# Exchanging transposed exponents between partition quadrants: per head through HBM, or per query block from SBUF to SBUF

## What is computed

```python
def attend_block(args):
    n, qn = args
    kw = lax.dynamic_slice_in_dim(kp, n * BLOCK, BLOCK + 2 * WINDOW, axis=1)
    vw = lax.dynamic_slice_in_dim(vp, n * BLOCK, BLOCK + 2 * WINDOW, axis=1)
    s_win = jnp.einsum('bqkgd,bjkd->bkgqj', qn, kw).astype(jnp.float32) * scale
    s_ctx = jnp.einsum('bqkgd,bjkd->bkgqj', qn, k_ctx).astype(jnp.float32) * scale
...
    logits = jnp.concatenate([sink_logits(sink, s_win.shape[:-1]), s_ctx, s_win], axis=-1)
    p = jax.nn.softmax(logits, axis=-1)
...
    return (jnp.einsum('bkgqj,bjkd->bqkgd', p_ctx, v_ctx)
            + jnp.einsum('bkgqj,bjkd->bqkgd', p_win, vw))
```

## Time and profile before

| | |
|---|---|
| median of three runs | 1405.53 us |
| profiled execution | 1405.84 us |
| its span in the trace | 1404.1 us |
| TensorE busy | 1367.9 us, 97% |
| VectorE busy | 864.5 us, 62% |
| ScalarE busy | 517.5 us, 37% |
| GpSimd busy | 74.8 us, 5% |
| the four heads | about 386 to 646 us |
| TensorE busy in them | 248.6 of 260 us |

### The profile page before, as it was taken

One profiled execution on the slowest core, in us unless ns is written; L12 is line 12 of the kernel. 1 busy time (PEld: TensorE's weight loads), 2 busy tenths in 40 slices (PEclk: granted clock), 3 DMA queues, 4 the chain that ended last, 5 costly groups with the idle time before them and its releaser, 6 DMA issues.

```text
span 1404.1 us, 19111 instructions
## 1 busy us (share of the span) xinstructions
PE 1367.9 (97%) x7258; PEld 1142.4 (81%) x7258; DVE 864.5 (62%) x1327; ACT 517.5 (37%) x798; POOL 74.8 (5%) x145
## 2 busy tenths in 40 slices
PE   5999999999999999999999999999999999999998
PEld 2788888888878788878888888888888888887887
DVE  6545655656787787776645776677665334474435
ACT  5323422234564645454222442212363223333332
POOL 0001111111000000000110100000000000010000
PEclk9999999999999999999999999999999999999999
DMA  9996567666676757687766666356533333365333
GB/s 384 407 396 250 180 206 254 191 186 198 201 208 163 192 172 178 176 230 261 236 198 192 195 192 194 92 173 195 160 91 102 103 91 105 105 198 181 111 90 120
DMA packets 103490, 265.35 MB, mean 189 GB/s; under 512 B 13536, under 2 KB 41200, under 8 KB 102000
## 3 DMA queue, kind: packets, MB, share of 16 engines
q1 hardware_dynamic: 81792, 185.72, 42.5%
q0 software_dynamic: 19936, 73.38, 16.7%
q10 hardware_dynamic: 1680, 5.10, 1.0%
HBM read 245.78 MB, written 18.38 MB: 188 GB/s over the span
## 4 chain that ended last, share of the span: by engine, by line
PE 83%; DMA 6%; DVE 5%; issue 2%; SPq 2%; ACT 2%; DVEq 0%; ACTq 0%
PE ps L1578 83%; DMA blocks<-cond_row 2%; DMA modchunk<-blocks 2%; DMA kvmem<-in_ctxT 1%; SPq L431 1%; DVE w_lo L972 1%; DVE pt_lo L1288 1%; DMA raw<-in_mod 1%; ACT w_hi L543 1%; DVE cond_row L1275 1%; DVE tmp L1265 0%; SPq L389 0%; DVE tmp L1098 0%; DVE kvmem L1160 0%; DVE kvmem L1265 0%
## 5 line engine op out<-in xcount | busy, mean ns | idle before, releaser
L1578 PE MATMUL ps<-h_hi,w_hi 128*128 128x512 f32 x1592 | 621.0, 390 | 2.1 <-DVE h_lo L1053 1.2
L1578 PE MATMUL ps<-h_lo,w_hi 128*128 128x512 f32 x1592 | 618.5, 389 | 0.0
L1578 PE MATMUL ps<-h_hi,w_lo 128*128 128x512 f32 x1592 | 618.2, 388 | 0.0
L972 DVE TENSOR_TENSOR w_lo<-raw,w_hi 128x1024 fp32r<-128x1024 f32 x206 | 252.2, 1224 | 371.2 <-ACT w_hi L543 370.3
L543 ACT CAST w_hi<-raw 128x1024 fp32r<-128x1024 f32 x206 | 216.1, 1049 | 598.8 <-PE ps L1578 598.7
L1578 PEld LDWEIGHTS ps<-h_hi,w_hi 128*128 128x128 f32 x1592 | 299.0, 188 | 65.8 <-issue 5.4
L1578 PEld LDWEIGHTS ps<-h_hi,w_lo 128*128 128x128 f32 x1592 | 298.9, 188 | 62.0
L1578 PEld LDWEIGHTS ps<-h_lo,w_hi 128*128 128x128 f32 x1592 | 299.0, 188 | 58.5
L978 DVE CUSTOM_DVE_ANT_0 modchunk<-modchunk,cond_row 128x1024 f32<-128x1024 f32 x128 | 154.6, 1219 | 19.9 <-DMA modchunk<-in_modb 19.7
L489 POOL DMA_DIRECT2D modchunk<-in_modb x128 | 67.6, 528 | 828.3 <-DVE modacc L978 811.9
L744 ACT ACTIVATE tmp<-tmp,stat 128x513 f32<-128x513 f32 (+1 forms) x24 | 18.7, 780 | 43.1 <-DVE stat L1265 43.0
(11 more groups left out here) (231 smaller groups left out, 1356.1 us busy)
## 6 DMA issues: line engine op xcount, KB each, us to landing
raw<-in_weights SPq DMA_DIRECT2D x208, 512.0 KB, 3.6
modchunk<-in_modb POOLq DMA_DIRECT2D x128, 512.0 KB, 4.7
raw<-in_mod SPq DMA_DIRECT2D x32, 512.0 KB, 9.2
modchunk<-in_mod SPq DMA_DIRECT2D x16, 512.0 KB, 7.5
cond_row<-in_mod SPq DMA_DIRECT2D x16, 512.0 KB, 9.5
blocks<-cond_row SPq DMA_DIRECT2D x24, 320.0 KB, 5.4
blocks<-cond_row SPq DMA_DIRECT2D x24, 256.0 KB, 2.9
modchunk<-blocks SPq DMA_DIRECT2D x64, 80.0 KB, 3.6
```

The source lines that it names most:

```text
L972: nc.vector.tensor_tensor(low, src, high.bitcast(F32), ALU.subtract).then_inc(lo_ready, 1)
L1578: return nc.tensor.matmul(out, lhsT, rhs, start=start, stop=stop, skip_group_check=True)
```

## The change

The transposed exponents of the three steps of a block are collected in one buffer (`cond_row`) and exchanged once a block, straight from SBUF to SBUF into a second one (`modchunk`). There are 16 transfers, one for each pair of source and target quadrant, of 32 partitions by 1536 bytes (blocks 0 and 3) or 1920 bytes (blocks 1 and 2). The four with equal source and target go on GpSimd's queue, the other twelve on SP's. The copy in HBM goes. High parts are made three at a time in slots 4, 7, 10 and 13, low parts three at a time in slots 5, 8, 11 and 14. With one buffer of each kind, `turn_blocks` of a block's first step waits until the transfers of the block before have landed, and in slots 6 and 12 it now stands behind the weights' low part. The inverse sums have one buffer instead of two.

```diff
-TURN_LAG = 3
-TURN_SLOTS = 3
+HIGH_SLOTS = (4, 7, 10, 13)
+LOW_SLOTS = (5, 8, 11, 14)
+ROW_SLOTS = (4, 7, 10, 13)
+POOL_MOVES = [(a, a) for a in range(4)]
+SP_MOVES = [(a, j) for j in range(4) for a in range(4) if (a, j) not in POOL_MOVES]
...
+        def block_source(n, a, j):
+
+            return block_runs(n, cond_row)[a * QUADRANT:(a + 1) * QUADRANT, j]
+
+        def block_target(n, a, j):
+
+            return block_runs(n, chunk_flat)[j * QUADRANT:(j + 1) * QUADRANT, a]
+
+        def moves_landed(eng, b):
+
+            eng.wait_ge(pt_landed, 16 * len(SP_MOVES) * (b + 1))
+            eng.wait_ge(pt_landed_pool, 16 * len(POOL_MOVES) * (b + 1))
...
-            def store_blocks(i, k):
-                g, cols = i * STEPS + k, key_tiles(k) * P
-                sp.wait_ge(turned, g + 1)
-                sp.dma_start(turn_scratch[g % 4, :, 0:cols], blocks_out[g % 2][:, 0:cols]).then_inc(written[g % 2], 16)
-
-            def fetch_blocks(i, k):
...
+            def move_blocks(i, n):
+                b = i * BLOCKS + n
+                sp.wait_ge(turned, (b + 1) * GQA)
+                if b:
+                    sp.wait_ge(pt_ready, b * GQA)
+                for a, j in SP_MOVES:
+                    sp.dma_start(block_target(n, a, j), block_source(n, a, j)).then_inc(pt_landed, 16)
...
                     if k < STEPS and k % GQA == GQA - 1:
+                        move_blocks(i, k // GQA)
                         store_inverse(i, k // GQA)
-                    if 3 <= k <= STEPS and k % GQA == 0:
-                        fetch_inverse(i, k // GQA - 1)
...
+            for b in range(KV_HEADS * BLOCKS):
+                pool.wait_ge(turned, (b + 1) * GQA)
+                if b:
+                    pool.wait_ge(pt_ready, b * GQA)
+                for a, j in POOL_MOVES:
+                    pool.dma_start(block_target(b % BLOCKS, a, j), block_source(b % BLOCKS, a, j)).then_inc(pt_landed_pool, 16)
...
-                if g >= 2:
-                    dve.wait_ge(written[g % 2], 16 * (g // 2))
-                nc.vector.transpose(blocks_out[g % 2][:, 0:cols].rearrange("p (j t c) -> p j t c", j=4, c=QUADRANT),
+                if k % GQA == 0 and g:
+                    moves_landed(dve, g // GQA - 1)
+                nc.vector.transpose(turned_blocks(k),
...
-                    if k > TURN_LAG:
-                        for n in {NEXT_SCORES: (STEPS - 2, STEPS - 1), NEXT_SCORES + 1: ()}.get(k, (k - TURN_LAG - 1,)):
-                            turned_lo(i, n)
+                    if k in LOW_SLOTS:
+                        for j in range(GQA):
+                            turned_lo(i, LOW_SLOTS.index(k) * GQA + j)
...
-                    if k < STEPS and (k or first):
+                    if k < STEPS and k % GQA:
                         turn_blocks(i, k)
                     if k < STEPS and k % GQA == GQA - 1:
                         invert_sums(i, k // GQA)
                     if k in UNIT_SLOTS:
                         lo(i + G_Z, UNIT_SLOTS.index(k) + 2)
+                    if k < STEPS and k % GQA == 0 and (k or first):
+                        turn_blocks(i, k)
                     if k in BLOCK_SLOTS:
                         block_out(i, BLOCK_SLOTS.index(k))
```

More of the change, by code:

```diff
@@ L277, in build @@
         chunk_flat = modchunk[:].rearrange("p a n -> p (a n)")
[L278 to L281, removed]
+        inverse_row = kv_part(k_rope + 5 * P + QUADRANT // 2, [GQA * P])
         key_raw = kv_part(k_rope, [2, COLS])
@@ L313, in turned_tiles, with block_runs, turned_blocks, landed_tiles @@
             return dst[:, 0:tiles, j * P:(j + 1) * P].rearrange("p t (a c) -> p t a c", c=QUADRANT)
-        def landed_tiles(i, k):
-            return blocks_in[(i * STEPS + k) % TURN_SLOTS][:, 0:key_tiles(k) * P].rearrange("p (a t c) -> p t a c", a=4, c=QUADRANT)
+        def block_runs(n, mem):
+            return mem[:, 0:GQA * key_tiles(n * GQA) * P].rearrange("p (a x) -> p a x", a=4)
+        def turned_blocks(k):
+            run = key_tiles(k) * QUADRANT
+            return block_runs(k // GQA, cond_row)[:, :, k % GQA * run:(k % GQA + 1) * run].rearrange("p a (t c) -> p a t c", c=QUADRANT)
+        def landed_tiles(k):
+            run = key_tiles(k) * QUADRANT
+            return block_runs(k // GQA, chunk_flat)[:, :, k % GQA * run:(k % GQA + 1) * run].rearrange("p a (t c) -> p t a c", c=QUADRANT)
+        def block_source(n, a, j):
[5 more added lines that the diff above has]
+            eng.wait_ge(pt_landed_pool, 16 * len(POOL_MOVES) * (b + 1))
         S_END = 6 * 512 - 256
@@ L352, in build @@
         exp_done, turned = sem("exp_done"), sem("turned")
-        written = [sem(f"written{i}") for i in range(2)]
-        pt_landed = [sem(f"pt_landed{i}") for i in range(TURN_SLOTS)]
+        pt_landed, pt_landed_pool = sem("pt_landed"), sem("pt_landed_pool")
         inverse_ready = sem("inverse_ready")
         inverse_written = [sem(f"inverse_written{i}") for i in range(2)]
-        inverse_landed = [sem(f"inverse_landed{i}") for i in range(2)]
+        inverse_landed = sem("inverse_landed")
         row_stored, row_back = sem("row_stored"), sem("row_back")
@@ L750, in turned_hi @@
                 g = i * STEPS + k
[L751 to L754, removed]
+                if k % GQA == 0:
+                    moves_landed(act, g // GQA)
+                    if g:
+                        act.wait_ge(pv_done, g // GQA)
+                nc.scalar.copy(turned_tiles(k, pt_hi), landed_tiles(k)).then_inc(pt_hi_ready, 1)
             def last_swap(i, k):
@@ L785, in attention @@
                         hi(i + G_Z, UNIT_SLOTS.index(k) + 2)
[L786 to L787 removed]
+                    if k in HIGH_SLOTS:
+                        for j in range(GQA):
+                            turned_hi(i, HIGH_SLOTS.index(k) * GQA + j)
                     if i < 2:
@@ L1287, in turned_lo @@
                 dve.wait_ge(pt_hi_ready, i * STEPS + (k + 1))
-                nc.vector.tensor_tensor(turned_tiles(k, pt_lo), landed_tiles(i, k), turned_tiles(k, pt_hi).bitcast(F32),
+                nc.vector.tensor_tensor(turned_tiles(k, pt_lo), landed_tiles(k), turned_tiles(k, pt_hi).bitcast(F32),
                                         ALU.subtract).then_inc(pt_ready, 1)
@@ L2066 @@
     out = nc.dram_tensor("out", (2, KT // 2, P, SEQ), F32, kind="ExternalOutput").ap()
-    blocks = nc.dram_tensor("blocks", (4, P, 5 * P), F32, kind="Internal").ap()
     inverses = nc.dram_tensor("inverses", (2, P, GQA), F32, kind="Internal").ap()
     row = nc.dram_tensor("row", (1, D), F32, kind="Internal").ap()
-    build(nc, *args, out, blocks, inverses, row)
+    build(nc, *args, out, inverses, row)
     result = run_bass_kernel_spmd(nc, [arrays], core_ids=[0]).results[0]["out"]
```

36 lines of the change are left out of this document (11 added, 25 removed).

## The result

The kernel after takes 1481.16 us (median of four runs, 1479.29 to 1486.85) against 1405.1 us before: a ratio of 1.054, 95% interval 1.051 to 1.058. It is slower, as forecast, but by 76 us instead of 40, and the time lies outside the range.

The account below looks back on a forecast made before the run. TensorE work plus its few waits was taken to bound the kernel. Twelve block intervals of 17.3 us, 207.6 against 165.4, lose 42 us; 2 come back: +40, 1445 us, range 1425 to 1472.

Parts of the forecast that it names:

- Eleven more issues ... at 0.44 that is 4.8 us: First queue after each closing transpose: eleven issues before the last transfer begins, 4.8 us of a 6.9 us wait.
- high end of 0.48: Slow case: 0.48 us an issue and 3.7 us landings give a 9.0 us wait, 2.1 more per interval: 1470.
- were not spread by it beyond 2.00 us: Earlier fetches also wrote quadrants, four issues taking at most 2.00 us, so the issue sets the pace.
- since nothing else stands in the queue then: Reason for taking 2.0 us from issue to landing for the block's last transfer on the first queue.
- the rest of those stretches stays: Between heads no transpose waits for landings, so apart from the 2 us counted back those stretches keep their time.
- 2 us back: Between heads: two or three slot 12 waits for low parts, 0.9 us each, go, winning 2 us.
- hidden wait: Rival 1: VectorE doesn't wait long and TensorE's ten waits go; at best 1394 us. Chance 0.05.
- half hidden: Rival 2: block interval of 13.8 to 14.2 us, offset by 2 us between heads; no change, 1405. Chance 0.04.
- Rival 4: Landings as slow as in the crowded queue, over 9 us of wait: above 1470. Chance 0.06.
- clock rival: Rival 3: TensorE's granted clock falls in the new intervals' gaps of about 3.8 us; 1460 to 1560. Chance 0.1.
- the granted clock falls in the gaps: One of three conditions under which the prediction called itself wrong; TensorE's gaps in the new block intervals.
- The other signs: Expected profile: twelve VectorE idles of 3 to 5 us, TensorE maxima waits of 3 to 4, closing transposes 16 to 19 apart.

Follow-up runs that it names:

- short rows: Kernel after, with the first queue's 12 transfers moving only 16 floats (64 bytes) of each row instead of 384 or 480: 1475.61 us, ratio 1.050.
- work in TensorE's gaps: Kernel after, plus ten extra matmuls into an unread PSUM bank before the scores of steps 5, 8 and 11 of each head: 1483.23 us, ratio 1.056.
- eight on each queue: Kernel after, with eight transfers on the first queue and eight on GpSimd's instead of 12 and 4: 1459.91 us, ratio 1.040.
- source in HBM: Kernel after, with the first queue's 12 transfers reading weight rows in HBM instead of the transposed exponents: 1453.35 us, ratio 1.034.
- four on the first queue: Kernel after, with four transfers on the first queue and four on GpSimd's, eight of 16 quadrant pairs not exchanged: 1419.21 us, ratio 1.011.
- the kernel before with the value product later: Kernel before, with the value product in slots 6, 9 and 12 behind two gate projection parts instead of one: 1403.82 us, ratio 0.998.

## Why the prediction was right and wrong

**Right: the sign and its mechanism.** The wait stood where the prediction put it, twelve times, and TensorE waited for the maximum behind it. The cut to four issues, the HBM source and the split over two queues each moved the interval by about what the chain says: forecast 14.7, 17.3 with 0.44 us an issue, and 17.0, measured in head 1 as 15.4, 17.7 and 17.3 us. The sums show it best. In the kernel after and in the runs that leave the place of the wait alone, the part up to the waiting transpose and the part behind it are, added over the twelve intervals:

| | wait part | rest |
|---|---|---|
| kernel after | 112.9 us | 122.6 us |
| short rows | 106.6 us | 122.6 us |
| work in TensorE's gaps | 114.2 us | 122.7 us |
| eight on each queue | 92.0 us | 122.7 us |
| source in HBM | 90.3 us | 122.7 us |
| four on the first queue | 57.3 us | 123.2 us |

The wait halves and the rest stays: every microsecond of wait is one of the interval. The rest was forecast as 12 x 10.4 = 124.8 us.

**Wrong: the term "Eleven more issues ... at 0.44 that is 4.8 us".** It was sized from issues whose one side is HBM, the nearest rows, and its high end of 0.48 was taken from the same rows. From SBUF to SBUF an issue takes 0.63 us with the gap, so eleven take 6.9. That is 2.1 us in each of twelve intervals, 25 of the 37 us of the span that were missed. 17.3 + 2.1 = 19.4 us an interval; the mean measured is 235.5 / 12 = 19.6. The landing was sized right: 2.0 us taken, 1.98 measured.

This term alone did not break the range. Its upper end allowed a wait of 9.0 us, for another reason (landings of 3.7 us), and stood at 1470; eleven waits of about 9.1 us would have fitted in it by luck. What took the time beyond it are the two that follow, which the prediction put at nothing or at a gain.

The statement that four fetches "were not spread by it beyond 2.00 us" holds for the lines of the earlier trace rows only. Right behind the store of 471.25 that is shown there, four of them took 3.06 us:

```profile
471.69 3.06 SPq L431 DMA_DIRECT2D modchunk<-blocks  x4
```

That these were slow for having a quadrant as target isn't shown; the first queue's other traffic is a rival.

**Wrong: landings of 2.0 us, "since nothing else stands in the queue then".** That holds for the first queue; the other queues were left out. In head 3 one interval, from 683.52 to 707.49 us, took 24.0 us, with a wait of 13.0. ScalarE's queue loads 1 MB of x there. Transfers from 676 to 700 us (KB each, us to landing):

```profile
main<-in_xT ACTq DMA_DIRECT2D x1, 1024.0 KB, 8.0
modchunk<-cond_row SPq DMA_DIRECT2D x12, 60.0 KB, 4.9
```

The landings took 4.9 us beside it instead of 2.0. The wait is 4 us longer than the 9.1 of the others, 4 us of the missed. With short rows, the same load issued 1.9 us after the closing transpose as here, the wait was 9.5 us, so the delay comes with the bytes of the exchange. That the load is the cause fits this but was not tried by moving it.

**Wrong: "the rest of those stretches stays", and 2 us back.** Outside the intervals 6.7 us were lost. 3.8 of them lie between the heads, and 2.8 of these are work of TensorE that slid there out of the intervals. That it slid because TensorE had run at half clock around each gap is supported by the run with work in the gaps, as shown there, and not tried by itself. Where the waits were shortest, with four issues, the stretches between heads took 71.5 us, 3.5 less than before: a gain as the prediction counted it is there when nothing overlays it. The 2.0 us after the last head can't be told from scatter, since that part took 769 to 775 us in all runs and 774.1 in the kernel before with the value product later; one wait of 3.8 us for low parts stands in it. With these 8.7 us, the 25 and the 4, the missed 37 us of the span are covered to within 1 us.

**The rivals.** A hidden wait and a half hidden one did not happen. Rival 4 gave the right side of the range, above 1470 with a wait over 9 us, for the wrong reason: all landings but those of one interval were fast. The clock rival did happen, as the lowered digits of the clock in the page and the mean of 0.91 over the heads show, and so did the sign "the granted clock falls in the gaps" that the prediction named as one of being wrong. Its price was wrong. It counted 1 us of scores on the chain each time, or TensorE's whole work at half clock. In seven of the twelve intervals the scores ran at half clock, in the other five the clock fell only a microsecond or two after TensorE was back, and with the clock mostly full again the time stayed. The first is an example of those five, scores at full speed after nearly 4 us:

```profile
404.50 0.44 PE L1596 MATMUL ps<-k_hi,q_hi 128*128 128x384 f32 x1 [3.90 <-DVE stat L1281]
```

The rule of the Trainium skill (TensorE: Matmul & The Clock Gate, "Part 1: The HAM clock gate") that the clock falls to 1.2 GHz after an idle stretch agrees with this trace: 0.50 after the gap of 4.1 us. A fall can still be nearly free, when another engine's chain is longer.

**The other signs.** Closing transposes were 17.7 to 24.0 us apart (16 to 19 forecast), the stalls on VectorE 5 to 11 us (3 to 5 forecast, low because the wait itself was). TensorE's gaps before the scores were 2.9 to 4.4 us and once 7.9 (3 to 4 forecast). GpSimd's four were in before the first queue's last, as forecast. The section on the change names slots 6 and 12 for a transpose behind the weights' low part; it is slot 6 alone, since the steps end with slot 11.

## What to carry to other kernels

Fewer bytes and one hop less are worth nothing when the price is a count of issues on one queue: count issues times their spacing plus one landing, and ask what is queued behind the wait for it. One buffer for a block's data turns that sum into a wait once a block, in front of everything that the waiting engine has next; moving the waiting instruction behind the work that others need adds no work and gave back 23 of 76 us. An exchange that is alone on its own queue can still be delayed by a load on another one. For an operation that the trace does not show, the bound must be widened in every factor that the new operation changes, here the kind of source, and not only in the one that looks uncertain.

## What the runs showed of the hardware

- An issue on SP's queue costs 591 ns (median) when source and target are in SBUF and 421 ns when the source is in HBM, for the same shape. It does not depend on the bytes (2 KB or 60 KB). A store from SBUF to HBM, of 128 rows, took 338 ns.
- A transfer of 60 KB from SBUF to SBUF lands 2.0 us after its issue, one of 2 KB after 1.8 us. Beside a load of 1 MB on another queue these were 4.9 and 3.3 us.
- GpSimd's queue issues such a transfer in 497 ns, faster than SP's 591, but paused for 3.3 us after the fifth of eight in the same interval of both runs that gave it eight.
- TensorE's granted clock fell to 0.50, 1.2 GHz, in or right behind each of the twelve gaps of 2.9 to 7.9 us, in five of them only when TensorE was back at work, and was full again 3 to 6 us after the gap. After six gaps of 1.8 to 2.3 us it fell in three.
